# Expert scores, second half: one wide matmul or two narrow ones in the same columns

## The reference, cut to what matters

```python
q = (xb @ w_q).reshape(B, T, PEER_HEADS, 2, PEER_DKEY // 2)
...
g = jax.nn.softmax(top_s, axis=-1)
u_sel = jnp.take(u_tab, idx, axis=0)
h = jnp.einsum('bthkd,btd->bthk', u_sel, xb)
a = (jax.nn.gelu(h.astype(jnp.float32)) * g).astype(xb.dtype)
return jnp.einsum('bthk,bthkd->btd', a, jnp.take(v_tab, idx, axis=0))
```

## Time and profile before

| | us |
|---|---|
| runs (3) | 1771.62 median, 1770.96 to 1772.96 |
| span of the profiled execution | 1769.9 |
| TensorE busy | 1744.5 (99%) |
| GpSimd busy | 1121.1 (63%) |
| VectorE busy | 996.1 (56%) |
| ScalarE busy | 952.5 (54%) |

### The profile page before, as it was taken

The page is one execution under the profiler, slowest core; times in us unless marked ns, Lnnn a source line. Parts: engine busy times, 40 slices in busy tenths (PEclk is TensorE's granted clock), DMA queues, the critical chain, the costliest instruction groups (busy, mean ns, idle before and its releaser), DMA issues.

```text
span 1769.9 us, 34694 instructions
## 1 busy us (share of the span) xinstructions
PE 1744.5 (99%) x13094; PEld 1540.6 (87%) x13094; DVE 996.1 (56%) x1915; ACT 952.5 (54%) x1426; POOL 1121.1 (63%) x496
## 2 busy tenths in 40 slices
PE   8999999999999999999999999999999999999998
PEld 6888899999999999888888878888888899978887
DVE  5225233992478888544444455465557963565555
ACT  5468454446544444545544557666567942346565
POOL 6956775888888888555455566665667431555653
PEclk9999999999999999999999999999999999999999
DMA  8544453555544444565566744465553411146552
GB/s 306 198 148 141 153 182 131 185 183 178 179 143 143 142 142 142 170 196 192 191 229 241 238 143 154 157 225 190 190 172 114 167 26 59 45 152 205 190 190 84
DMA packets 68099, 292.66 MB, mean 165 GB/s; under 512 B 13184, under 2 KB 13712, under 8 KB 50464
## 3 DMA queue, kind: packets, MB, share of 16 engines
q1 hardware_dynamic: 67808, 291.12, 49.0%
q10 hardware_dynamic: 144, 0.07, 0.0%
q0 software_dynamic: 48, 0.08, 0.0%
HBM read 289.14 MB, written 1.05 MB: 164 GB/s over the span
## 4 chain that ended last, share of the span: by engine, by line
PE 81%; POOL 9%; issue 5%; ACT 2%; DVE 2%; DMA 1%; POOLq 0%; SPq 0%; DVEq 0%; ACTq 0%
PE bank L1060 8%; POOL rows_lo L2971 7%; PE bank L876 7%; PE bank L1081 6%; PE bank L938 6%; PE bank L1196 6%; PE bank L941 6%; PE bank L935 6%; PE bank L1064 4%; PE bank L882 4%; PE bank L618 4%; PE bank L624 4%; PE bank L619 4%; PE bank L908 3%; PE bank L647 1%
## 5 line engine op out<-in xcount | busy, mean ns | idle before, releaser
L2956 POOL TENSOR_TENSOR unit_lo<-unit_raw,unit_hi 128x2048 fp32r<-128x2048 f32 (+1 forms) x86 | 332.2, 3882 | 129.9 <-ACT unit_hi L1645 116.6
L2971 POOL TENSOR_TENSOR rows_lo<-rows_raw,rows_hi 128x1024 fp32r<-128x1024 f32 x128 | 309.5, 2419 | 85.0 <-ACT rows_hi L1765 46.0
L2998 POOL TENSOR_TENSOR a_lo<-table,a_hi 128x256 fp32r<-128x256 f32 x128 | 178.5, 1395 | 159.9 <-ACT a_hi L1844 159.8
L2573 DVE TENSOR_TENSOR rows_lo<-rows_raw,rows_hi 128x1024 fp32r<-128x1024 f32 x128 | 161.7, 1263 | 185.6 <-ACT rows_hi L1840 185.6
L1840 ACT ACTIVATE rows_hi<-rows_raw 128x1024 fp32r<-128x1024 f32 x128 | 135.6, 1060 | 168.4 <-PE bank L941 168.4
L3028 POOL TENSOR_TENSOR up_lo<-up_raw,up_hi 128x2048 fp32r<-128x2048 f32 x22 | 110.8, 5036 | 156.6 <-ACT up_hi L1916 127.1
L1645 ACT ACTIVATE unit_hi<-unit_raw 128x2048 fp32r<-128x2048 f32 x70 | 134.0, 1919 | 65.9 <-PE bank L624 35.4
L1060 PE MATMUL bank<-x_lo_hi,up_hi 128*128 128x512 f32 x640 | 159.8, 392 | 0.2 <-DVE acc L2666 0.2
L882 PE MATMUL bank<-x_lo_hi,rows_lo 128*128 128x256 f32 x1024 | 143.2, 282 | 0.5 <-POOL rows_lo L2971 0.5
L882 PEld LDWEIGHTS bank<-x_lo_hi,rows_lo 128*128 128x128 f32 x1024 | 135.7, 190 | 6.6 <-POOL rows_lo L2971 0.9
L938 PE MATMUL bank<-rows_hi,a_lo 128*128 128x512 f32 x512 | 138.5, 391 | 0.8 <-POOL a_lo L2998 0.8
(11 more groups left out here) (498 smaller groups left out, 3956.7 us busy)
## 6 DMA issues: line engine op xcount, KB each, us to landing
unit_raw<-in_ring SPq DMA_DIRECT2D x70, 1024.0 KB, 4.9
rows_raw<-in_u SPq DMA_DIRECT2D x128, 512.0 KB, 3.6
rows_raw<-in_v SPq DMA_DIRECT2D x128, 512.0 KB, 3.5
up_raw<-in_up SPq DMA_DIRECT2D x44, 1024.0 KB, 5.2
down_raw<-in_down SPq DMA_DIRECT2D x22, 1024.0 KB, 4.9
unit_raw<-in_ring SPq DMA_DIRECT2D x20, 256.0 KB, 3.6
const<-in_const SPq DMA_DIRECT2D x1, 1792.0 KB, 14.8
X<-in_x SPq DMA_DIRECT2D x2, 512.0 KB, 5.8
```

Source lines behind the costliest of these rows:

```text
L2573: V.tensor_tensor(rows_lo[q][:, :], rows_raw[q][:, :], rows_hi_f[q % 2], ALU.subtract).then_inc(S("v_lo_ready"), 1)
L2956: return nc.gpsimd.tensor_tensor(unit_lo[SLOT_OF[n]][:, w], unit_raw[SLOT_OF[n]][:, w], hi, ALU.subtract)
L2971: nc.gpsimd.tensor_tensor(rows_lo[q][:, :], rows_raw[q][:, :], rows_hi_f[q % 2], ALU.subtract).then_inc(S("u_lo_ready"), 1)
L2998: nc.gpsimd.tensor_tensor(a_lo[q % 2][:, :], table[:, i * ROWS_RING + q, :], a_hi_f[q % 2], ALU.subtract).then_inc(S("a_lo_ready"), 1)
```

## The change

In the second half TensorE uses the same two narrow matmuls as in the first, into the same 256 columns. The copy of the left half (64 on ScalarE) and the sum of the halves (64 on VectorE) are gone, with their two semaphores, and the gelu waits for TensorE alone. The last gelu of the stage keeps its place on ScalarE. Loads, gates, and the stage after are as they were.

```diff
-            def hidden(t, q, first, wide=False):
+            def hidden(t, q, first):
...
                 for k in range(KT):
-                    if wide:
-                        mm(o[:, :], hi[:, k, :], x_both(k), start=k == 0, stop=False, skip_group_check=True)
-                    else:
-                        mm(o[:, SEQ:], hi[:, k, :], xu_hi[:, k, :], start=k == 0, stop=False)
-                        mm(o[:, SEQ:], hi[:, k, :], x_lo[:, k, :], start=False, stop=False)
+                    mm(o[:, SEQ:], hi[:, k, :], xu_hi[:, k, :], start=k == 0, stop=False)
+                    mm(o[:, SEQ:], hi[:, k, :], x_lo[:, k, :], start=False, stop=False)
                 pe.wait_ge(S("u_lo_ready"), t + 1)
                 for k in range(KT):
-                    m = mm(o[:, SEQ:], lo[:, k, :], xu_hi[:, k, :], start=False, stop=k == KT - 1, skip_group_check=wide)
+                    m = mm(o[:, SEQ:], lo[:, k, :], xu_hi[:, k, :], start=False, stop=k == KT - 1)
...
-            def hidden_lo_part(t, q):
+            def hidden_gelu_late(t, q, first=False):
 
                 act.wait_ge(S("hidden_filled"), t + 1)
-                A(hidden_lo[:, :], PS[q % 4][:, 0:SEQ], ACT.Copy).then_inc(S("hidden_lo_ready"), 1)
-
-            def hidden_gelu_of_sum(t, q, first=False):
-
-                act.wait_ge(S("hidden_added"), t - (HALF_TILES - 1))
                 if not first:
                     act.wait_ge(S("hidden_in_table"), t - HALF_TILES)
                 A(hidden_act[:, :], PS[q % 4][:, SEQ:], ACT.Gelu_apprx_tanh).then_inc(S("hidden_used"), 1)
...
                     act.wait_ge(S("hidden_filled"), t - 1)
-                    if not narrow:
-                        hidden_lo_part(t - 2, (q - 2) % ROWS_RING)
                     act.wait_ge(S(f"u{q}_loaded"), i * 16 + 16)
...
-            def hidden_sum(m, q):
-
-                ve.wait_ge(S("hidden_lo_ready"), m + 1)
-                o = PS[q % 4][:, SEQ:]
-                V.tensor_tensor(o, o, hidden_lo[:, :], ALU.add).then_inc(S("hidden_added"), 1)
-
             def gates_into_table(n, q, first=False, second=False, last=False):
 
-                if not first:
-                    hidden_sum(n - 1, (q - 1) % ROWS_RING)
                 ve.wait_ge(S("gates_filled"), n + 1)
...
-            hidden_sum(N_KEYS - HALF_TILES - 1, ROWS_RING - 1)
```

More of the change, by code:

```diff
@@ L262, in build @@
     x_both = lambda k: x_lo_hi[:, :, k * SEQ:(k + 1) * SEQ]
-    hidden_lo = view("hidden_lo", K12_AT, [SEQ])
     hidden_act = view("hidden_act", U_AT + D * (ROWS_RING - 1), [SEQ])
@@ L914, in _ @@
                 gate_group(q, q)
-                hidden(HALF_TILES + q, q, False, wide=True)
+                hidden(HALF_TILES + q, q, False)
             with pe.Fori(HALF_ROUND + 1, N_KEYS // ROWS_RING) as i:
@@ L918, in _ @@
                     gate_group(i * ROWS_RING + (q - HALF_TILES), q)
-                    hidden(i * ROWS_RING + q, q, False, wide=True)
+                    hidden(i * ROWS_RING + q, q, False)
             for c in range(TC):
@@ L1820, in half_round @@
                     else:
-                        hidden_gelu_of_sum(t - 2, (q - 2) % ROWS_RING, first and q == 2)
+                        hidden_gelu_late(t - 2, (q - 2) % ROWS_RING, first and q == 2)
             half_round(HALF_ROUND, True)
@@ L1825, in _ @@
                 half_round(i)
-            hidden_lo_part(N_KEYS - 2, ROWS_RING - 2)
-            hidden_gelu_of_sum(N_KEYS - 2, ROWS_RING - 2)
+            hidden_gelu_late(N_KEYS - 2, ROWS_RING - 2)
             if upto < 4:
@@ L1845, in output_round @@
                     if first and q == 0:
-                        hidden_lo_part(N_KEYS - 1, ROWS_RING - 1)
-                        hidden_gelu_of_sum(N_KEYS - 1, ROWS_RING - 1)
+                        hidden_gelu_late(N_KEYS - 1, ROWS_RING - 1)
                     if first and q == 2:
```

## The result

The changed kernel takes 1778.34 us (median of 8 runs, 1775.42 to 1780.88), the kernel before on the same chip 1772.95 us (8 runs, 1770.96 to 1773.92). The ratio is 1.0029, with a 95% interval of 1.0019 to 1.0040: slower, as forecast. The time lies 0.3 us above the predicted range.

What follows compares the result with a forecast made beforehand. TensorE's start-to-start spacing was taken to bound the kernel: 1771.62 us, with +5.1 us for the tiles and -1.1 us at the stage's end (+4.0), gave 1775.6 us, range 1773.0 to 1778.0.

Steps and rivals of the forecast that it cites:

- TensorE sets the pace, and a pair costs more than a wide matmul: Second half: TensorE never idles; two narrow matmuls cost 240 ns where a wide one costs 231.
- the tile's term: Second half on TensorE: 80 ns more in each of 64 tiles, +5.1 us, bounds +3.6 and +5.4.
- the gain behind another kind: Gate group's rows: a narrow matmul may gain a few ns, so 80 ns a tile instead of 82 to 85.
- The 85 ns of the stage without gates: Up-projection's 2.795 us against the first half's tile of 24 narrow matmuls, 2.880: upper bound for a tile's growth, +5.4 us.
- The Trainium skill's spacing rule: Second half's matmuls spaced N/2.4 + 2.5 ns: splitting costs 1.3 us, total 1771.8 us; under the no-change rival, 5%.
- The end of the stage: First two output tiles: without the last copy and addition ahead, -1.1 us, bounds -0.3 and -1.1.
- What is late next is that a_lo, if anything is: Second output tile: GpSimd's a_lo might be the next operand to come late, by 0.1 us.
- Copy and sum are free in the loop: Second half: ScalarE's 0.38 us copy and VectorE's 0.43 us addition a tile are hidden beside TensorE; removal gains nothing.
- Pairs with the same weights are no cheaper: Rival for the 16 new matmuls: pairs with repeated weights run at 111 ns a matmul, total 1765.9 us; 4%.
- gap once in eight tiles: Rival in TensorE's longer loop body: code loaded anew at six jumps back, +7 us, total 1782.8 us; 6%.
- The rule on jumps back beyond two pages: TensorE's loop: a taken jump beyond two pages of 256 instructions stalls, though TensorE has room for 2048.
- The sum: Second half plus start of the output stage: +5.1 - 1.1 = +4.0 us, bounds +2.5 and +5.1.

Runs made afterwards that it cites:

- Narrow_kept: The changed kernel with a copy and an operation of the same sizes kept on ScalarE and VectorE; 1777.97 us, ratio 1.0026 to the kernel before.
- wide_no_sum: The changed kernel with the wide matmuls put back, still without copy and sum; 1771.96 us, ratio 0.9996 to the kernel before.
- last_narrow: The kernel before with narrow pairs for the last of its 128 tiles alone, which has no copy and sum; 1772.08 us, ratio 0.9992.
- grouped: The changed kernel with eight high-part matmuls, then eight low-part ones, in all 128 tiles, so no neighbours share weights; 1776.19 us in one run.
- the two repeats: The changed kernel measured twice more, unedited; 1776.97 us, ratio 1.0020, and 1777.15 us, ratio 1.0027, to the kernel before.
- own_columns: The kernel before with each second-half wide matmul split into two narrow ones writing separate bank halves, copy and sum kept; 1778.05 us in one run.

## Why the prediction was right, and where it was wrong

- **TensorE sets the pace, and a pair costs more than a wide matmul: right.** 3.767 us a tile (forecast 3.77), no idle time, 241.05 us for the window (forecast 241.4). Narrow_kept and wide_no_sum took the two sides of the change apart, and only TensorE's moved the tile.
- **Size of the tile's term: +5.1 us forecast, +4.7 measured.** The step that was off is "Then a pair costs 2 x 120 = 240 ns where the wide one costs 231. Per tile 8 x 9 = 72 ns." The sixteen narrow matmuls took 62 ns more than the eight wide ones, since the first pairs behind the gates start closer than 120 ns, 8 ns in sum. The low part rose by 11 ns (forecast 10), and the gate group's starts stayed within 0.1 ns. Together 73 ns, where I took 80: the gain behind another kind was foreseen as "a few ns" and was 9 of the 82. The 85 ns of the stage without gates didn't carry over. The likely reason: there the change takes away both changes of kind of a tile, here one of three.
- **The Trainium skill's spacing rule: the measurement decides.** By N/2.4 + 2.5 ns (the Trainium skill, TensorE: Matmul & The Clock Gate, section Back-to-back issue gap) the stage would have grown by 1.3 us; it grew by 4.7. The trace has 120.0 ns for 256 columns with their weight load.
- **The end of the stage: right.** -1.1 us forecast, -1.02 measured, and shown by last_narrow to hang on the last sum. "What is late next is that a_lo, if anything is" came true as well: the second output tile still takes 2.754 us, 0.03 too long, and its starts turn uneven at the first use of `a_lo`.
- **Copy and sum are free in the loop: right**, 3.693 us without them.
- **Rivals.** Pairs with the same weights are no cheaper (grouped). No gap once in eight tiles appeared: every tile takes 3.766 or 3.767 us, so the longer loop body had no cost; code came in 72 pieces once and in 71 in the two repeats. The rule on jumps back beyond two pages (the Trainium skill, Runtime: NRT & Kernel Launch, section Instruction fetch mechanics) did not bite here; its larger figure for TensorE's room fits.
- **The sum: right within 0.3 us for the stage** (+4.0 against +3.7). **The range failed**, at its last step: "The runs before lie up to 1.3 us from their median, so I add about 1.1 to 1.3 us on either side". Three runs showed too little of the spread. Over 29 runs on one chip the kernel before ranges from 1770.55 to 1776.11 us with a median of 1773.44, 1.8 us above the median that I started from (other chips: 1773.90 and 1772.41), and the changed kernel's three medians spread over 1.4 us themselves (1776.97 to 1778.34). From the 1775.6 us of the forecast to the 1778.34 measured, the start makes +1.3 us (1772.95 for 1771.62), the stage -0.3 and the rest +1.7. Start plus stage, 1776.6 us, was inside the range; the 1.7 us came from outside the stage, where single executions of one and the same kernel differ by up to 3.7 us (701.4 to 705.1). Nor is time less span the fixed 1.7 us of the forecast: with each run's own span it is 2.1 or 2.2 us in most and up to 3.9 us in some, in both kernels. That the three differences exceed the stage's by 0.9 us on average stays unexplained.

## What to carry to other kernels

Where one engine has no idle time, price a change by the distance of its starts, not by busy time or by how many instructions it frees elsewhere: 44 us of work left the other two engines here and the tile didn't notice. A matmul of 512 columns was cheaper here than two of 256, by 13 ns in a stream of one kind and by some 8 ns in the mixed tile, so take work off TensorE's instruction count before taking it off idle engines, and look for an idle engine's last instruction at a stage's border, the one place where it was on the path here. An operand that comes just late may show no idle time but only uneven starts, as in output tile 1: look at the starts one by one. Before giving a range, ask how far medians of few runs lie apart, and add that to the bounds of the sum.

## What the runs showed of the hardware

- A matmul with its own weight load costs 120.0 ns at 256 columns and 227 ns at 512, at the full clock. Twice 256 columns thus cost 13 ns more than 512 in a stream of one kind; in this mixed stage the split of eight cost 62 ns, 8 ns a pair. Neither repeated weights (grouped) nor the columns of the bank that are written (own_columns) alter it.
- Where the kind of matmul changes (width, or float32 against the faster format), the next starts are uneven before they settle: behind the gates 118, 119, 121, 117 and 118 ns and then 120.0, 8 ns less in sum; 512 columns behind 256 take 233, 236, 228, 233 and 231 ns and then 227, 27 ns more. It repeats in every tile within 2 ns. The same 233 to 231 come without any change of kind where an operand seems to come just late (output tile 1, +34 ns). What in the engine makes them is not shown.
- Reading the moving columns in two far pieces of 256 costs a wide matmul nothing that a tile shows: 3.693 us with two pieces and with one.
- With the same idle time of 1.7 us ahead, one execution got the clock at 0.5 for 3.4 us and another none; it cost 1.6 us in line 1108. Four of the twelve profiles have such a stretch.
